# Where a float32r matmul's operands lie in SBUF: the buffers of the weight ring 64 bytes apart modulo 512

## What is computed

```python
# first block: 8-head MoBA attention, 8-head MLA attention, gates, MLP
proj = rms_norm(x) @ w_in                      # 1024 x 4256
q, kv = rms_norm(c_q) @ w_uq, rms_norm(c_kv) @ w_ukv
merged = gate_a * (o_a @ w_branch_a) + gate_b * (o_b @ w_branch_b)
x = x + rms_norm(merged @ w_out)
x = x + rms_norm(square(relu(rms_norm(x) @ w_up)) @ w_down)   # 1024 x 4096 x 1024
# second block: spatial gating, dilated attention, and experts (PEER)
proj = rms_norm(x) @ w_in_2
x = x + concat(rms_norm(a), rms_norm(b)) @ w_out_2
q = rms_norm(x) @ w_query                      # top 16 of 16384 experts for each of 8 heads
x = x + sum(softmax(s) * gelu(x . expert_u[e]) * expert_v[e])
return rms_norm(x)
```

## Time and profile before

| | |
|---|---|
| median of 3 runs | 1277.93 us |
| the profiled execution's own time | 1279.17 us |
| its span, first to last instruction | 1277.3 us |
| TensorE busy with matmuls | 1266.1 us (99%), 7351 records |
| VectorE busy | 994.9 us (78%) |
| ScalarE busy | 741.4 us (58%) |
| share of TensorE in the chain that ended last | 93% |
| granted TensorE clock, mean | 0.999 of 2.4 GHz |

### The profile page before, as it was taken

How to read it: one execution, slowest core, us unless ns; L and a number is a source line. 1 busy time by engine, 2 the same in 40 slices (tenths; PEclk the granted TensorE clock), 3 DMA queues, 4 the chain that set the end, 5 groups by cost and what they waited for, 6 DMA issues and landing times.

```text
span 1277.3 us, 19726 instructions
## 1 busy us (share of the span) xinstructions
PE 1266.1 (99%) x7351; PEld 1098.2 (86%) x7351; DVE 994.9 (78%) x1861; ACT 741.4 (58%) x1289; POOL 34.7 (3%) x29
## 2 busy tenths in 40 slices
PE   9999999999999999999999999999999999999998
PEld 8899988888878889988888888888888888888886
DVE  6776568884457867999999788888888888876666
ACT  6666457654446655455555666666666666654554
POOL 0000031000011001000000000000000000000000
PEclk9999999999999999999999999999999999999999
DMA  8533455655556436488888765656598888877763
GB/s 265 169 128 123 142 187 182 193 189 195 183 164 224 133 116 202 149 287 290 290 274 299 256 190 192 213 185 200 184 330 285 287 287 296 273 246 275 244 241 114
DMA packets 77406, 277.19 MB, mean 217 GB/s; under 512 B 8768, under 2 KB 9536, under 8 KB 77056
## 3 DMA queue, kind: packets, MB, share of 16 engines
q1 hardware_dynamic: 75840, 272.03, 64.4%
q0 software_dynamic: 1040, 3.34, 0.8%
q10 hardware_dynamic: 432, 0.56, 0.1%
HBM read 249.16 MB, written 26.74 MB: 216 GB/s over the span
## 4 chain that ended last, share of the span: by engine, by line
PE 93%; DVE 3%; ACT 1%; DMA 1%; POOL 1%; issue 0%; SPq 0%; DVEq 0%; ACTq 0%
PE ps L1144 27%; PE ps L549 23%; PE ps L530 16%; PE ps L552 11%; PE ps L539 3%; PE ps L538 3%; PE ps L540 3%; PE ps L1104 2%; PE ps L596 1%; PE ps L583 1%; POOL wlo L2516 1%; PE ps L589 1%; DMA raw<-in_w_in_c_dram 1%; ACT whi L1181 1%; PE ps L1063 1%; PE ps L577 1%
## 5 line engine op out<-in xcount | busy, mean ns | idle before, releaser
L1714 DVE TENSOR_TENSOR wlo<-raw,whi 128x1024 fp32r<-128x1024 f32 (+2 forms) x410 | 497.7, 1216 | 211.5 <-ACT whi L1181 206.9
L1181 ACT ACTIVATE whi<-raw 128x1024 fp32r<-128x1024 f32 (+2 forms) x421 | 442.1, 1051 | 359.0 <-PE ps L1144 147.2
L549 PE MATMUL ps<-turned_x,whi 128*128 128x512 f32 x1264 | 321.1, 396 | 0.0
L1144 PE MATMUL ps<-whi,turned_x 128*128 128x512 f32 x1024 | 315.7, 389 | 0.0
L549 PEld LDWEIGHTS ps<-turned_x,whi 128*128 128x128 f32 x1264 | 225.7, 188 | 39.3
L1144 PEld LDWEIGHTS ps<-whi,turned_x 128*128 128x128 f32 x1024 | 192.2, 188 | 40.2 <-DVE wlo L1714 0.2
L1144 PE MATMUL ps<-wlo,turned_x 128*128 128x512 f32 x512 | 199.2, 389 | 0.0
L552 PEld LDWEIGHTS ps<-turned_x,wlo 128*128 128x128 f32 x1264 | 170.1, 188 | 13.0
L552 PE MATMUL ps<-turned_x,wlo 128*128 128x256 f32 x1264 | 173.2, 278 | 0.0
L1144 PEld LDWEIGHTS ps<-wlo,turned_x 128*128 128x128 f32 x512 | 96.1, 188 | 19.9
L530 PE MATMUL ps<-whi,turned_x 128*128 128x512 f32 x328 | 106.6, 397 | 1.0 <-DVE wlo L1714 1.0
(11 more groups left out here) (331 smaller groups left out, 1537.8 us busy)
## 6 DMA issues: line engine op xcount, KB each, us to landing
raw<-in_expert_u_dram SPq DMA_DIRECT2D x128, 512.0 KB, 4.4
raw<-in_expert_v_dram SPq DMA_DIRECT2D x128, 512.0 KB, 4.7
acts<-stage SPq DMA_DIRECT2D x47, 512.0 KB, 5.2
raw<-in_w_up_dram SPq DMA_DIRECT2D x32, 512.0 KB, 3.5
raw<-in_w_down_dram SPq DMA_DIRECT2D x32, 512.0 KB, 4.3
stage<-acts SPq DMA_DIRECT2D x29, 512.0 KB, 5.8
raw<-in_w_in_dram SPq DMA_DIRECT2D x20, 512.0 KB, 4.1
X<-acts SPq DMA_DIRECT2D x18, 512.0 KB, 6.2
```

Of the source, the lines that this page charges most:

```text
L549: e.matmul(ps[b][:, :], whi[:, h, k * 128:k * 128 + 128], x[:, k, :, :], start=k == 0, stop=False)
L1144: m = e.matmul(ps[bank4(t, d)][:, :], x[:, n % 8, sl], w[:, h, d * 512:d * 512 + 512], start=n == 0 and k == 0, stop=n == 127 and k == 2)
L1181: e.activation(whi[:, u % NH, 0:n], raw[:, u % NR, 0:n], ACT.Copy).then_inc(*hi(u))
L1714: e.tensor_tensor(wlo[:, u % NH, 0:n], raw[:, u % NR, 0:n], whi[:, u % NH, 0:n].bitcast(F32), ALU.subtract).then_inc(*lo(u))
```

## The change

The two halves of the weight ring become one tile, `halves`, whose buffers are 2064 columns long instead of 2048, so that each buffer starts 64 bytes further on modulo 512 than the one before it. `turned_x` loses 64 bytes, and `T` and `R` change places: `T` now starts the tile and `R` lies 64 bytes behind it. The constants and statistics move ahead of it (`st` is 64 bytes longer), gaps are put in and taken out among the tiles of the four stages, and `cut` waits for all of EU's last unit from chunk 3 on (`R`'s chunk 3 now reaches into `T`'s chunk 4). No instruction is added, removed or moved on any engine, and each has its shapes as before.

```diff
         X = sb(ctx, "X", [128, 2, 1024])
         raw = sb(ctx, "raw", [128, NR, 1024])
-        whi = sb(ctx, "whi", [128, NH, 1024], F32R)
-        wlo = sb(ctx, "wlo", [128, NH, 1024], F32R)
-
-
-        turned_x = sb(ctx, "turned_x", [128, 4096 + 32], F32R)
-        T, R = (turned_x[:, a:a + 4096].rearrange("p (k h n) -> p k h n", h=2, n=256) for a in (16, 0))
+
+        halves = sb(ctx, "halves", [128, NH, 2064], F32R)
+        whi, wlo = halves[:, :, 0:1024], halves[:, :, 1024:2048]
+        cst = sb(ctx, "cst", [128, CST_W])
+        ppc = sb(ctx, "ppc", [128, PPC_W])
+        st = sb(ctx, "st", [128, 464])
+
+
+        turned_x = sb(ctx, "turned_x", [128, 4096 + 16], F32R)
+        T, R = (turned_x[:, a:a + 4096].rearrange("p (k h n) -> p k h n", h=2, n=256) for a in (0, 16))
...
-        cst = sb(ctx, "cst", [128, CST_W])
-        ppc = sb(ctx, "ppc", [128, PPC_W])
-        st = sb(ctx, "st", [128, 448])
...
         sg = sb(p1, "sg", [128, 16, 256])
+        sb(p1, "gap_o", [128, 48])
         OAh = sb(p1, "OAh", [128, 4, 256], F32R)
...
         OBl = sb(p1, "OBl", [128, 4, 256], F32R)
+        sb(p1, "gap_c", [128, 16])
         CQh = sb(p1, "CQh", [128, 3, 256], F32R)
...
-        sb(p2, "gap2", [128, 16])
         MH = sb(p2, "MH", [128, 32, 256], F32R)
...
-        sb(p3, "gap3", [128, 16])
         AH = sb(p3, "AH", [128, 4, 256], F32R)
...
                 if i >= 8:
                     e.wait_ge(*used.at(EV + i - 8))
-                elif i >= 4:
+                elif i >= 3:
                     e.wait_ge(*used.at(EU + 127))
                 else:
                     e.wait_ge(*half_used.at("u"))
```

## The result

The changed kernel takes 1289.51 us (median of 3 runs, 1288.92 to 1289.61) against 1277.93: a ratio of 1.0088, 95% interval 1.0065 to 1.0111. The forecast was 1283.4 with a range of 1269.5 to 1290.5 and 0.62 on slower. Direction and mechanism held; the size is twice the forecast of +5.5 us.

A forecast was written before the change was run, and what follows sets the result against it. The prediction took TensorE, busy 99% of the span, as the bound, with matmul pace set by operand places. Its terms summed to +5.5 us on the median of 1277.93, giving 1283.4 us, range 1269.5 to 1290.5.

The forecast's parts named there:

- I therefore sort the paces by offset: Matmul pace follows place of operand loaded minus place streamed, modulo 512: 226.7 ns at 0, 233.3 at +64.
- Item 1: EV's 1536 matmuls, offset 0 before, get 0, -64 and -128, 512 each: +4.4 us.
- dearer still: Rival: unseen offsets at 233.3 ns, slow 256-column matmuls, and every buffer step breaking the even pace: 1290.3 us, chance 0.18.
- Item 2: w_in_2's 240 matmuls get the same three offsets as EV's: +0.7 us.
- Items 3 and 4: Wide columns: 1264 matmuls of 512 columns go from -64 to +64, +128, +192, +2.6 us; 1264 of 256, 0.
- Item 5: The other 912 matmuls of 256 columns, mostly at 117.8 ns: 0, taken as the upper end.
- Items 6 to 8: Rows from T -0.7 us, w_down -1.1, AH and CKh together -0.2, all from new offsets.
- first test: First check of the mechanism: w_down should get faster, to 229.5 ns a matmul on average.
- Items 9: The wait of `cut` for chunk 3 behind EU's last unit: 0; without cover, under 1 us, once.
- 10: Constants, statistics, X, raw and stage, touched only by ScalarE, VectorE and DMAs, which have slack: 0.
- The place doesn't matter: Rival: the paces go with something else of the stages, so the change does nothing: 1277.9 us, chance 0.13.
- T in front lets the wide columns run free: Rival: in EU's wide columns load and stream fall into step, units take 2.72 us: 1270.8 us, chance 0.25.

The follow-up runs named there:

- run 2: The changed kernel with all ring buffers at one place modulo 512, the halves still interleaved: 1274.99 us, and 1275.15 us when repeated (ratio 0.9975).
- run 7: Kernel with ring buffers at one place and T at two: low halves moved 128 or 64 bytes behind the high ones, 1291.76 us and 1289.56 us.
- run 8: The kernel before with ring buffers in 64-byte steps and, in EV, R's chunk stepping along with them: 1284.86 us, EV 352.44 us.
- run 5: Three kernels with all ring buffers at 128 and other constant places for T, R, MH and AH: 1282.33, 1298.26 and 1288.27 us.

## Why the forecast was right, and where it fell short

- **What bounds the kernel**: right. Only TensorE's pace moved; VectorE and ScalarE did not.
- **"I therefore sort the paces by offset"**: right, 226.7 against 233.3 ns for EV with R 16 bytes further on. The modulus was wrong: 256, not 512. By the Trainium skill TensorE waits for nobody and loads take nothing from the stream ("TensorE: Matmul & The Clock Gate", part 2, and "SBUF — State Buffer", "Who interferes with whom"); these runs disagree, with those two numbers, and the measurement decides.
- **Item 1, EV, +4.4**: the term that was too small. I gave each matmul the pace of its own offset at once. Buffer 0 was to cost 0 and costs 48 ns a unit, buffer 1 43 instead of 32, buffer 2 75 instead of 70. The stage paid 7.1 us. Such a run-in stands in the earlier trace rows, behind an interruption; I had seen it, priced it at 20 ns a unit and put it into the rival "dearer still", whose 1290.3 us is the nearest of the four numbers. It belonged in the sum: it was in a row. That the rival came so near is in part luck: it also had every unseen offset at 233.3 ns (+128 and +192 were faster) and +3.2 us for the 256-column matmuls (measured +1.1). And the range holds the result only because it was stretched to this rival; the forecast's own 1277 to 1289 does not.
- **Item 2, w_in_2, +0.7**: measured +0.6.
- **Items 3 and 4, wide columns, +2.6 and 0**: +4.4 together. With 512 columns +64, +128 and +192 ran at 232.9, 232.0 and 230.2 ns, run-in included, mean 231.7 against the 231.4 forecast and 229.0 (not 229.4) before, +3.4. The 256-column ones went from 116.6 to 117.5, +1.1: taken as 0 on the ground that their pace alternated at one offset, while their mean does depend on it.
- **Item 5**, 0: +0.24, the gates and branches 0.2 us faster and w_query 0.5 slower.
- **Items 6 to 8, -2.0**: about -0.6. w_down got its 0 and -64, but with a run-in each time: 230.6 and 230.5 ns instead of 226.7 and 229.4. My "first test", w_down at 229.5 on average, came out at 231.3: the sign right, two thirds of the gain gone.
- **Items 9**, the wait of `cut`, **and 10**: nothing to be seen; the EV stage of run 2, which has both, is that of before to 0.03 us.
- **Rivals.** "The place doesn't matter" is out. "T in front lets the wide columns run free" was wrong for 512 columns (T in front at an even +64: 232.9) and half right for 256 (114.5, with a ring that does not step). Without its ring step the change is a gain of 3 us: against before, the profile of run 2 has w_down at -2.0, the gates and w_query at -1.8, the other rows stages at -1.3, and w_up and EU, faster in 256 columns and slower in 512, at +1.9.

Open: by what mechanism a load and a stream slow each other. "Own load" and "next load" both fail alone (runs 7 and 8), and the 6.7 ns for each change of place, fitted to run 7, gave 349.0 us for run 8, which took 352.4.

## To carry to other kernels

Where TensorE is the bound and float32r matmuls, each with a load of its own, follow each other without a gap, put what is loaded and what is streamed at the same place modulo 256 bytes for 512 streamed columns, and the loaded operand 64 bytes on (+64) for 256, the best of the places tried. Where the two alternate, as in the wide columns here, -64 gave the best total of those tried; measure it. Keep that place the same for every buffer of a ring and every chunk: with a ring in steps of 64 bytes EV ran at 231.4 ns a matmul, with a constant -64 w_down ran at 229.0 (run 5). Read the starts, not the durations: the pace is the difference of two start times over the count, and a line that runs at two paces in two stages is a hint that its operands' places matter.

## Not expected of the hardware

- The pace of a float32r matmul with 512 columns takes values from 226.7 to 233.3 ns by nothing but the place of its operands, was the same 256 bytes on (EV 348.48 us at 256, 348.46 at 0), and is as bad at 16 bytes as at 64.
- With 256 columns the order is another: 113.4 to 114.5 ns at +64, 119.1 to 120.0 at 0.
- The best and the worst pace of 512 columns are 6.7 ns apart, 16 cycles at 2.4 GHz; EV's 1536 matmuls took 348.5 us at the one and 358.6 at the other.
- The disturbance outlives the matmul: one step of 64 bytes was felt in about ten matmuls behind it, within one kernel each time in the same sequence of gaps but for 1 or 2 ns.
